# Reading the moving operand of single-pass float products backwards, and shifting the weight blocks by lines of 16 bytes

## The reference

```
def sqrelu_mlp(h, w1, w2):
    return jnp.square(jax.nn.relu(h @ w1)) @ w2

        m_lat = (silu_c @ ada_w[i] + ada_b[i]).reshape(B, N_MOD, 1, D)
        h_lat = modulate(rms_norm(x_lat, norm_g[i, 0]), m_lat[:, 0], m_lat[:, 1])
        y_ctx, y_lat = mla_mixer(h_ctx, h_lat, rope, need_ctx, ...)   # layer 1: gla_mixer
        x_lat = x_lat + m_lat[:, 2] * rms_norm(y_lat, norm_g[i, 1])
        h = modulate(rms_norm(x_lat, norm_g[i, 2]), m_lat[:, 3], m_lat[:, 4])
        x_lat = x_lat + m_lat[:, 5] * rms_norm(sqrelu_mlp(h, mlp_w1[i], mlp_w2[i]), norm_g[i, 3])
```

## Time and profile before

| what | value |
|---|---|
| median of 2 runs | 1960.31 us |
| span of the profiled execution | 1959.2 us |
| TensorE matmul busy | 1919.3 us, 10285 matmuls |
| TensorE weight loads busy | 1607.6 us |
| VectorE busy | 1400.5 us |
| ScalarE busy | 895.7 us |
| GpSimd busy | 250.2 us |
| moved by DMA | 315.12 MB, 161 GB/s on average |

### The profile page before, as it was taken

The page is one execution under the profiler, slowest core; times in us unless marked ns, Lnnn a source line. Parts: engine busy times, 40 slices in busy tenths (PEclk is TensorE's granted clock), DMA queues, the critical chain, the costliest instruction groups (busy, mean ns, idle before and its releaser), DMA issues.

```text
span 1959.2 us, 27475 instructions
## 1 busy us (share of the span) xinstructions
PE 1919.3 (98%) x10285; PEld 1607.6 (82%) x10285; DVE 1400.5 (71%) x2243; ACT 895.7 (46%) x1536; POOL 250.2 (13%) x332
## 2 busy tenths in 40 slices
PE   8999999999999999999999999999999999989998
PEld 4877788888888777889988888888888878878997
DVE  5898777888866655487997676767755567667765
ACT  3433355333343453576554224634233454557654
POOL 2101010211111200411101001101110021331000
PEclk9999999999999999999999999999999999999999
DMA  8434235655663451367875422655555245327763
GB/s 311 138 98 136 76 98 185 211 184 174 201 185 100 158 168 33 95 225 257 271 245 165 151 97 69 200 162 183 161 172 161 78 148 176 98 92 229 228 196 116
DMA packets 191827, 315.12 MB, mean 161 GB/s; under 512 B 14637, under 2 KB 114312, under 8 KB 191696
## 3 DMA queue, kind: packets, MB, share of 16 engines
q1 hardware_dynamic: 162512, 210.09, 33.0%
q0 software_dynamic: 29184, 103.29, 17.1%
HBM read 312.29 MB, written 1.05 MB: 160 GB/s over the span
## 4 chain that ended last, share of the span: by engine, by line
PE 82%; DVE 9%; issue 4%; ACT 2%; DMA 2%; POOL 1%; SPq 0%; DVEq 0%; POOLq 0%; ACTq 0%
PE bank L723 24%; PE bank L730 22%; PE bank L729 22%; PE bank L733 8%; DVE w L2242 3%; DVE acc L2267 2%; PE bank L728 2%; PE bank L726 2%; ACT junk L1642 1%; PE bank L785 1%; DMA raw<-in_mlp_w 1%; POOL st L3258 1%; PE bank L809 1%; DVE X L2386 1%; ACT w L1610 1%
## 5 line engine op out<-in xcount | busy, mean ns | idle before, releaser
L1610 ACT ACTIVATE w<-raw 128x1024 fp32r<-128x1024 f32 (+4 forms) x390 | 399.1, 1031 | 555.8 <-PE bank L730 481.8
L2242 DVE TENSOR_TENSOR w<-raw,w 128x1024 fp32r<-128x1024 f32 (+3 forms) x372 | 439.2, 1189 | 229.2 <-ACT w L1610 228.8
L723 PE MATMUL bank<-HH,w 128*128 128x256 f32 (+1 forms) x1552 | 509.5, 328 | 3.4 <-DVE HH L2369 2.0
L729 PE MATMUL bank<-HL,w 128*128 128x512 f32 (+1 forms) x1232 | 412.1, 334 | 0.0
L730 PE MATMUL bank<-HH,w 128*128 128x512 f32 (+1 forms) x1232 | 411.9, 334 | 0.0
L2267 DVE SCALAR_TENSOR_TENSOR acc<-ada,sc,acc 128x512 f32<-128x512 f32 x518 | 362.4, 746 | 2.3
L723 PEld LDWEIGHTS bank<-HH,w 128*128 128x128 f32 x1552 | 291.0, 188 | 30.5 <-issue 4.4
L723 PE MATMUL bank<-w,UH 128*128 128x512 f32 x768 | 300.7, 392 | 0.3 <-DVE UL L2544 0.3
L730 PE MATMUL bank<-w,UL 128*128 128x512 f32 x768 | 299.1, 390 | 0.0
L729 PE MATMUL bank<-w,UH 128*128 128x512 f32 x768 | 298.9, 389 | 0.0
L729 PEld LDWEIGHTS bank<-HL,w 128*128 128x128 f32 x1232 | 230.2, 187 | 26.1 <-issue 0.2
(11 more groups left out here) (354 smaller groups left out, 2610.1 us busy)
## 6 DMA issues: line engine op xcount, KB each, us to landing
raw<-in_mlp_w SPq DMA_DIRECT2D x256, 512.0 KB, 4.4
ada<-in_mod_w POOLq DMA_DIRECT2D x96, 512.0 KB, 4.5
ada<-in_ada_w POOLq DMA_DIRECT2D x80, 512.0 KB, 4.7
raw<-in_ml_w_qkvo SPq DMA_DIRECT2D x28, 512.0 KB, 3.7
raw<-in_conv_w_in SPq DMA_DIRECT2D x24, 512.0 KB, 4.2
raw<-in_ada_w SPq DMA_DIRECT2D x12, 512.0 KB, 6.1
raw<-in_mla_w_o SPq DMA_DIRECT2D x8, 512.0 KB, 3.9
raw<-in_gla_w_v SPq DMA_DIRECT2D x8, 512.0 KB, 4.0
```

The costliest lines, as they stand in the source:

```text
L723: pe.matmul(o, sh, mh, start=start, stop=False, skip_group_check=True)
L729: pe.matmul(o, sh, ml, start=False, stop=False, skip_group_check=True)
L1610: act.activation(k.halves(n)[0], k.raw[(NDIRECT + n) % NRAW][:, 0:m], ACT.Copy).then_inc(*k.w_hi.up("w hi", n))
L2242: dve.tensor_tensor(low, k.raw[(NDIRECT + n) % NRAW][:, 0:m], high.bitcast(F32), ALU.subtract).then_inc(*k.w_lo.up("w lo", n))
```

## The change

In `mm3` the output and both moving operands are taken with their columns in reverse, `x[:, ::-1]`. The first column that streams is the last one of the operand, and its result goes to the last column of the output; the same numbers land in the same places. Products outside `mm3` are as they were.

The shift of 8 bytes for blocks under 256 columns is gone. Instead every block of a part of the network begins `PLACE` numbers behind the buffer's start: 12 (48 bytes) in the latent attention's blocks up to its output projection, 0 from that output projection through layer 0's MLP and all of layer 1 (GLA and its MLP), 4 (16 bytes) in the convolution's layer, 8 (32 bytes) in the mLSTM's layer. The buffers grow from 2050 to 2064 numbers and the pads shrink, and no tensor other than the tiny `sc` and `minus_half` and the pads themselves changes its address.

```
-NARROW_AT = 2
+ROOM = 16
+PLACE = {"first": 0, "conv": 4, "gla": 0, "mlstm": 8, "latent": 12}
...
 def weight_stream(A):
+    at = [0]
+
     def wide(block):
-        return block, 0
+        return block, at[0]
...
-                yield W[kk:kk + 512, cb:cb + 256].rearrange("(k p) n -> p k n", p=128), NARROW_AT if narrow else 0
+                yield W[kk:kk + 512, cb:cb + 256].rearrange("(k p) n -> p k n", p=128), at[0]
...
+    at[0] = PLACE["latent"]
     yield from rows256(A["mla_w_dq"][0])
...
+    at[0] = PLACE["first"]
     yield from tokw(A["mla_w_o"][0], 0, D, 0, D)
...
+    at[0] = PLACE["gla"]
...
+    at[0] = PLACE["conv"]
...
+    at[0] = PLACE["mlstm"]
...
-            self.pair.append(sb(f"w{i}", [128, 2048 + NARROW_AT], F32R))
+            self.pair.append(sb(f"w{i}", [128, 2048 + ROOM], F32R))
...
     def mm3(o, st, mv, start, stop, late=None):
 
         sh, sl = st
-        mh, ml = mv
+        o, mh, ml = [x[:, ::-1] for x in (o, *mv)]
         pe.matmul(o, sh, mh, start=start, stop=False, skip_group_check=True)
```

More of the change, by code:

```diff
@@ L544, in lay_out @@
         for i in range(NSPL):
-            self.pair.append(sb(f"w{i}", [128, 2048 + NARROW_AT], F32R))
+            self.pair.append(sb(f"w{i}", [128, 2048 + ROOM], F32R))
             if i == 0:
                 self.sc, self.minus_half = sb("sc", [128, 4, 8]), sb("minus_half", [128, 16])
-            sb(f"w_pad{i}", [128, 8 if i == 0 else 56])
+            else:
+                sb(f"w_pad{i}", [128, 48])
         self.ada = [sb(f"ada{i}", [128, 2, 512]) for i in range(NADA)]
```

## The result

The kernel after took 1999.29 us, the median of 2 runs (1997.89 and 2000.69), against 1960.31 before. The ratio is 1.0199 with a 95% interval of 1.018 to 1.0219. It is slower beyond doubt; whether by more than 2% this measurement doesn't tell.

What follows compares the result with a forecast made beforehand. TensorE's start-to-start distance in `mm3` matmuls was taken as the bound, paid in full. The terms gave 1959.2 + 0 + 11.7 + 0 = 1970.9, with 1.1 us between span and median 1972 us; 8-in-10 range 1885 to 2030.

Steps and rivals of the forecast that it cites:

- Step (1): Reversed columns in `mm3`: direction itself costs 0 us; 512 columns stay at 226 to 228 ns in layer 0's MLP.
- The bound from above: Reversal in `mm3`: at most 240 ns per 512 columns, 13 ns more than usual, 72 us more in all.
- Step (2): Blocks under 256 columns in `mm3`: losing the 8-byte shift costs 4.2 ns each over 2784 matmuls, +11.7 us.
- The signed test: 256 columns in layer 1's MLP: about 120 ns expected; the 8-byte term is wrong if they keep 115.7.
- Step (3): Blocks shifted by 16, 32 and 48 bytes (latent attention, convolution's, mLSTM's layers): cost taken as 0, bounds 0 and 18 us.
- the reads stay together: Slower rival, `mm3`: the stream catches up with the load and waits; 235 to 240 ns, 2044 us in full; chance 0.19.
- Two cycles per column: Much slower rival, `mm3`: each backward column costs two cycles, 427 ns for 512 columns, about 3330 us; chance 0.07.
- the extra goes: Faster rival, `mm3`: the extra time per matmul vanishes, in full 80.7 us less, 1885 us after give-back; chance 0.30.
- Nothing happens: Rival, `mm3`: extra and shift are only a matter of width, 1960 us; no chance of its own given.

Runs made afterwards that it cites:

- e1: Kernel before with output and moving operands of `mm3` reversed, blocks where they lay, 8-byte shift kept: 2001.56 us against 1960.62 for the kernel before.
- e2: Kernel before with only the moving operands of `mm3` reversed, output written forward: 2005.12 us against 1960.62 for the kernel before.
- e3: Kernel before with only the output of `mm3` reversed, moving operands read forward: 1960.48 us against 1960.62 for the kernel before.
- e7: Streams of 27 matmuls on TensorE alone, varying read order, places and load size; 512 columns: 226.7 ns in a two-dimensional forward pattern, 233.3 with 16-byte lines backward.
- e4: Streams of 48 matmuls on TensorE alone, varying width, direction, stationary shift and width, and type; 512 columns: 226.9 ns forward, 233.3 backward.
- e8: Kernel after, read forward with every block at place 0, so only the 8 bytes are gone: 1967.52 us against 1963.41 for the kernel before.
- e5: Kernel after with outputs and moving operands of `mm3` forward again, new places kept: 1980.55 us against 1962.01 for the kernel before.
- e11: Backward streams on TensorE alone at 64 places within 256 bytes: least distance 559.9 cycles for 512 columns, 282.6 for 256.
- e6: Kernel before with the 8-byte shift set to 0, which also moved tensors by multiples of 32 bytes: 1991.93 us against 1962.01 for the kernel before.
- e10: Kernel before with 64 bytes of shift at 1824 matmuls of 256 columns, 8 bytes kept at 960: 1962.86 us against 1961.90, ratio 1.0005.

## Why the prediction was wrong

**What bounds the kernel** held. The distance between matmuls of `mm3` is paid in full: (233.3 - 226.8) x 5472 = 36 us by the two timelines, 33 us by the sum over all of them, since some stretches stood above the typical figure already before, as in the earlier trace rows (227.3 ns on average, 233.3 after). The total moved by 39.

**Step (1), the reversal itself at 0, is the step that failed.** Its test, "wrong if 512 columns take other than 226 to 228 ns in layer 0's MLP", came out at 233.3, and the 5 ns in layer 0 at which the prediction as a whole fails were passed too. The term of the sum that stood at 0 measured 33 us. e1 has the loss without any other part of the change, e2 and e3 put it on the read. The argument was that "a direction changes neither how many lines are read nor how many results are written". Both halves are true and beside the point: what counts is the order of the lines (e7), at equal number. The short loads of the earlier trace rows were read as "the number of meetings is not what the 32 cycles count", and that also is right: a load of one column leaves 231.9 ns (e7). But from "not a count" I went on to "not sensitive to direction", which no row said. The same had 230.8 ns, 4 ns over the rest, with half of the pieces misplaced. It was put aside as small, when it was a sign that 544 cycles were a special case with something to lose. (Its cause need not be the misplaced pieces: loads of 32 columns, none of them misplaced, have 231.7 ns in e4.) The bound from above held, but its 240 ns are one distance between two rounded starts: the twelve matmuls from 72.14 to 74.89 us have 229 ns on average. DVE's equal scans said nothing about TensorE.

**Step (2), the 8 bytes, had the right mechanism, and its term holds only forward.** The sum had +11.7 us; read forward, removing them costs 11.1 us in the 256 columns (e8), of which the span shows 6.5. In the kernel after, the term is another, because the two edits don't add:

| us in steady matmuls | of 512, with the 44 by ones | of 256 |
|---|---|---|
| before | 1253.4 | 322.3 |
| places new, 0 everywhere, forward (e8) | 1253.5 | 333.4 |
| places of the kernel after, forward (e5) | 1268.1 | 331.1 |
| reversal alone, 8 bytes kept (e1) | 1286.5 | 333.7 |
| after | 1286.6 | 328.8 |

Backward, the 8 bytes do harm: 119.9 ns in e1, 118.3 after. So once `mm3` reads backward, taking them away and setting the new places saves 4.9 us. Between before and after, both together cost 6.5 us in the 256 columns, which the prediction had as 11.7. The signed test held in part: layer 1 went from 115.7 to 118.3, not to 120.

**Step (3), the places at 0, came out right for a reason that it didn't have.** After the change the convolution's layer and layer 0 are alike (233.6 and 233.3), the mLSTM's and layer 1 too (117.8 and 118.3). But forward, the same places cost 14.6 us in the 512 columns (e5 against e8), inside its bound of 18, which I had left to the range. They cost nothing here since backward reading has 560 cycles at 0, 16, 32 and 48 bytes alike (e11). That is luck, not foresight.

**The sum.** By its own steps and the measured prices it is 1959.2 + 33.2 (1) + 6.5 (2) + 0 (3) = 1998.9, the span of the profiled execution, against 1959.2 + 0 + 11.7 + 0. The other rows of the table on the result nearly cancel. The wide range, up to 2030 us, holds the result only by the half of the slower rival that it took in.

**The rivals.** The nearest was *the reads stay together*: it asked for 235 to 240 ns and put the point that decides at 39 us, where the result lies, and it was right that forward and backward differ by how the reads of a matmul go. Its mechanism, a faster stream that catches up with the load, isn't shown: the distance does not rise with the load's size, and no place within 256 bytes lets the two miss each other going backward (e11). *Two cycles per column* would be 427 ns, and *the extra goes* in full 216 (226.8 less 11.0); both were clearly off. *Nothing happens* fell with e1.

**The rules that were weighed.** The Trainium skill, SBUF — State Buffer, Who interferes with whom, gives TensorE two read ports and has it wait on no one. The runs contradict its use here: with the other engines silent, moving only the stationary part by 16 bytes takes a stream from 226.9 to 233.3 ns (e4). Measured, the place and direction of TensorE's own two reads are not free for fp32r. The Trainium skill, PSUM — Partial Sum Buffer, Specifications, warns of non-contiguous access patterns for matmuls; for a result written with a step of -1 the trace doesn't agree, 226.8 ns in e3 as before. The Trainium skill, TensorE: Matmul & The Clock Gate, Back-to-back issue gap, lists 518 cycles for 512 columns; bf16 has them (215.8 ns, e4), and fp32r, which this kernel runs, has 544.

**What stays open.** Why a backward order of the 16-byte lines costs 16 cycles in 512 columns and nothing at 320, and what the first 32 cycles over the 512 columns are. Whether the moving read pays by itself or only beside a weight load: no run read backward without a load before each matmul, and none read the stationary operand backward. Nothing beyond 256 bytes of relative place was varied for the backward read, and no other widths of load for it than those of e4.

## What to carry to other kernels

When a stream runs close to one column in each cycle, the distance from start to start is the number to watch, and it depends on the order in which the operand's 16-byte lines are read and on where the two operands begin relative to each other. Read the moving operand forward, reverse on the output side if something must be reversed, and give each buffer its padding so that an edit of one buffer doesn't move the others (some 24 us in e6). What an edit is worth in one direction says little about it in the other: in the matmuls of 256 columns the 8 bytes gained 11 us forward and lost 5 against the new places backward, so price such edits together, not one by one. And a gain or loss in the matmuls can shrink in the time: of the 11 us the span showed 6.5.

## What the hardware showed that I had not expected

- No steady stream of 512 fp32r columns was under 544 cycles (226.7 ns). Backward streams have 560 (233.3) or more; forward ones with the operands apart lie between 544 and 576 (240.0); backward runs of four 16-byte lines have 640. Bf16 has 518 in either direction.
- A forward stream with the stationary part 16 bytes off and a backward stream cost the same 560 cycles, and both together also cost 560 (e4). Of the six places tried there, only 128 bytes takes the backward stream to 239.8 ns (576).
- A load of a single column leaves the stream of 512 columns no shorter a distance than one of 128 at the same place: 231.9 against 226.7 ns (e7).
- The same code with the blocks at the same place ran at 113.4 ns in one stretch of 96 matmuls and at 117.7 in the one before it (e10).
- 320 columns have 352 cycles in either direction, while 288, 352 and all wider ones that were tried pay 4 to 16 cycles for going backward.
